# ScalarE's sigmoid visit per pair of heads in a gated linear recurrent layer, made in two parts one slot apart

## Chip, core and metric

One core of a Trainium2 chip runs the whole program: one launch, no other core busy. The metric is device time in microseconds (us). Engines: TensorE (PE; its weight loads are PEld), VectorE (DVE), ScalarE (ACT), GpSimd (POOL), and SyncE (SP), which only issues DMAs here.

## What is computed

A trunk of four layers with 384 token rows (256 of a prompt, 8 streams of 16). Each layer is a token mixer followed by a gated feed-forward net, both closed by a residual and a layer norm. The mixers are forgetting attention (layers 0 and 3), a gated linear recurrence (layer 1) and causal pooling (layer 2). The change lies in layer 1 alone:

```python
def hgrn_chunk_step(S, inp):
    q, k, v, g = inp
    b = jnp.cumsum(g, axis=1)
    decay = jnp.exp(jnp.where(causal, b[:, :, None] - b[:, None, :], -jnp.inf))
    scores = jnp.einsum('bthc,bshc,btshc->bhts', q, k, decay)
    o = jnp.einsum('bhts,bshv->bthv', scores, v) + jnp.einsum('bthc,bhcv->bthv', q * jnp.exp(b), S)
    S_new = jnp.exp(b_last)[..., None] * S + jnp.einsum('bshc,bshv->bhcv', k * jnp.exp(b_last[:, None] - b), v)

q, fx, iv, gate = jnp.split(x @ w_in, 4, axis=-1)
q = jax.nn.silu(q)
log_f = jnp.log(lb + (1.0 - lb) * jax.nn.sigmoid(fx))
k = (1.0 - lb) * jax.nn.sigmoid(-fx)
o = o * lax.rsqrt(jnp.mean(jnp.square(o), axis=-1, keepdims=True) + RMS_EPS) * norm_g
o = o.reshape(B, T, D_MODEL) * jax.nn.silu(gate)
return o @ w_out, S_final
```

There are 8 heads of 128 channels. For each pair of heads four sigmoids are wanted: of `q`, of `fx`, of `-fx`, and of `gate`; and one logarithm.

## The kernel before

Each engine runs a program of its own, written out by hand, and the programs meet only at semaphores. An engine works its list strictly in order, so a wait in it holds up everything behind it. The sets of functions for which ScalarE has tables differ: sigmoid is in one, logarithm and exponential in another, and each change of set is an `ACT_TABLE_LOAD` (copy and square run with either).

Weights stream through a ring of six buffers in units of 256 rows by 512 columns (`w_raw`, 128 x 1024). SyncE loads a unit when the unit six places ahead of it has been used (`unit_used`), ScalarE rounds it to `w_hi` (`w_hi_of`, L386), VectorE writes the rest to `w_lo` (`w_lo_of`, L676), and TensorE makes three products of them (`unit_fm`, `unit_tm`).

The recurrent layer (`hgrn`) runs in slots, a loop over `u` that every engine has (L579 of ScalarE, L1019 of VectorE, L1841 of TensorE). Slots 0 to 31 hold one unit of the input projection each, eight for each pair of heads `g`: four (`u % 8` below 4) for queries and forget values, four for values and gates. Beside them run the steps of the heads: head `h` begins its sums of logarithms in slot 6 + 4h and its products in slot 10 + 4h (`phases`). What the change and the prediction touch:

- **Slot 8g + 4.** ScalarE copies the queries to `q_g` (L586), VectorE the forget values to `f_r` (L1025). At the slot's end ScalarE runs `sigmoids(g)` (L513): the load of the sigmoid tables, the sigmoids of queries (`sg_q`), of forget values (`g_s`), of their negatives (`k_g`) and of the gates of the pair before (`sg_g`, from `g` = 1 on), the load of the log and exp tables, then two logarithms over `g_s`.
- **Slot 8g + 5.** VectorE runs `results(h)` for `h` = 2g - 2 (L992). It waits for the finished gate (L1005) and multiplies the head's output by it (L1008). Behind it in its list stand `sample_states`, then `state_sides(2g - 1)`, which writes `k2` (L946, L948), then `w_lo`, then the multiply of `q_g` by `sg_q` and of `k_g` by a constant (L1059, L1062). ScalarE runs two exponentials (L554) and one `w_hi`.
- **Slot 8g + 6.** TensorE opens with `turn_keys(2g - 1)` (L1765), which waits for `k2` (L1767), then `turn_logs(2g)`, which waits for the logarithms (L1738), then the slot's unit. ScalarE copies the turned logarithms to `gT_hi` (L595), VectorE subtracts them to `gT_lo` (L1045), and `sums` in slot 8g + 7 waits for both (L1749).
- **GpSimd** finishes gates in `gates(g)` (L1338): it waits for the semaphore `sgg` and makes two multiplies (L1342, L1345).
- In slot 33 `sigmoids(GRP)` makes the last pair's gate sigmoid alone.

Of the kernel before, what the change touches and what calls it, by code (L numbers as in the profile page):

```python
# [22 lines left out]
ACT = mybir.ActivationFunctionType  # L23
# [36 lines left out]
GRP = HG // 2  # L60
# [28 lines left out]
def trunk_program(nc, x_prompt, x_sample, cache_fox_k, cache_fox_v, cache_fox_lf, state_hgrn, cache_pool,  # L89
# [8 lines left out]
    with ExitStack() as ctx:  # L98
# [31 lines left out]
        lb_col = sb("lb_col", [P, KD], after("lbT"))  # L130
        oml_col = sb("oml_col", [P, KD], after("lb_col"))
# [135 lines left out]
        def at(mark, value):  # L267

            return mark[0], value + mark[1]
# [108 lines left out]
        def _(act):  # L378
# [131 lines left out]
            def hgrn(i, j):  # L510
                f, m0, out0 = HGR[i], START[i]["mix"], START[i]["out"]

                def sigmoids(g):  # L513

                    if g < GRP:
                        act.wait_ge(*at(f["f_ev"], g + 1))
                        act.wait_ge(*at(f["q_ev"], g + 1))
                        act.wait_ge(*at(f["qk"], g))
                        nc.scalar.activation(sg_q[:, :, :], q_g[:, g % 2, :, :], ACT.Sigmoid)
                        act.wait_ge(*at(f["gT"], 2 * g))  # L520
                        nc.scalar.activation(g_s[:, :, :], f_r[:, :, :], ACT.Sigmoid)
                        nc.scalar.activation(k_g[:, g % 2, :, :], f_r[:, :, :], ACT.Sigmoid, scale=-1.0).then_inc(f["sig"][0], 1)
                    if g:
                        act.wait_ge(*at(f["t01_ev"], g))
                        act.wait_ge(*at(f["t2_ev"], g))
                        act.wait_ge(*at(f["gate"], 2 * g - 2))
                        nc.scalar.activation(sg_g[:, :, :], gate[:, (g - 1) % 2, :, :], ACT.Sigmoid).then_inc(f["sgg"][0], 1)
                    log_exp_table()
                    if g < GRP:
                        act.wait_ge(*at(f["sig"], g + 1))  # L530
                        for e in range(2):
                            h = 2 * g + e
                            nc.scalar.activation(g_s[:, e, :], g_s[:, e, :], ACT.Ln, bias=lb_col[:, h:h + 1],
                                                 scale=oml_col[:, h:h + 1]).then_inc(f["g"][0], 1)

                def exps(h, first):

# [41 lines left out]
                for u in range(SLOTS):  # L579
                    (ha, ka), (hb, kb) = phases(u)  # L580
                    g = u // 8
                    if u % 8 == 4 and g < GRP:
                        act.wait_ge(unit_used, m0 + u)
                        if g >= 2:
                            act.wait_ge(*at(f["o"], 2 * g - 2))
                        nc.scalar.activation(q_g[:, g % 2, :, :], ps[:, FM_BANK[g]:FM_BANK[g] + 2, 0:T], ACT.Copy).then_inc(f["q_ev"][0], 1)  # L586
                    if u % 8 == 0 and 1 <= g <= GRP:
                        act.wait_ge(unit_used, m0 + u)
                        nc.scalar.activation(vo[:, 0:2, 2 * P * (g - 1):2 * P * g], ps[:, 4:6, 0:2 * P], ACT.Copy)
                        nc.scalar.activation(gate[:, (g - 1) % 2, 0:2, :], ps[:, 4:6, 2 * P:4 * P], ACT.Copy).then_inc(f["t01_ev"][0], 1)  # L590
                    if kb == 0:
                        turned_keys(hb)
                    if ka == 0:
                        act.wait_ge(*at(f["gT"], ha + 1))
                        nc.scalar.activation(gT_hi[:, :], ps[:, 0, 0:T], ACT.Copy).then_inc(f["gT_hi"][0], 1)  # L595
                    if kb == 2:
                        squares(hb)
                    if ka is not None and ka >= 1:
                        exps(ha, 2 * ka - 2)
                    for h in TURN_AT.get(u, ()):  # L600
                        turned_out(h)
                    if 1 <= u <= 8 * GRP:
                        w_hi_of(m0 + u - 1 + RING)
                    if u - 2 in OUT_AT:
                        w_hi_of(out0 + OUT_AT[u - 2] + RING)
                    if u % 8 == 4 and g < GRP:
                        sigmoids(g)
                    if u == 8 * GRP + 1:
                        sigmoids(GRP)
                turned_out(HG - 1)  # L610
                for u in range(len(OUT_AT), 2 * CU - TAIL):
                    w_hi_of(out0 + u + RING)
# [55 lines left out]
        def _(dve):  # L668
# [241 lines left out]
            def hgrn(i, j):  # L910
# [108 lines left out]
                for u in range(SLOTS):  # L1019
                    (ha, ka), (hb, kb) = phases(u)  # L1020
                    g = u // 8
# [32 lines left out]
                        w_lo_of(m0 + u - 1 + RING)  # L1054
                    if u - 2 in OUT_AT:
                        w_lo_of(out0 + OUT_AT[u - 2] + RING)
                    if u % 8 == 5 and g < GRP:
                        dve.wait_ge(*at(f["sig"], g + 1))
                        V.tensor_tensor(q_g[:, g % 2, :, :], q_g[:, g % 2, :, :], sg_q[:, :, :], ALU.mult)  # L1059
                        for e in range(2):  # L1060
                            h = 2 * g + e
                            ins = V.tensor_scalar(k_g[:, g % 2, e, :], k_g[:, g % 2, e, :], oml_col[:, h:h + 1], None, ALU.mult)  # L1062
                        ins.then_inc(f["qk"][0], 1)
# [102 lines left out]
        def _(pool):  # L1166
# [102 lines left out]
            def hgrn(i, j):  # L1269
# [67 lines left out]

                def gates(g):  # L1338

                    pool.wait_ge(*at(f["sgg"], g + 1))  # L1340
                    v = gate[:, g % 2, :, :]
                    G.tensor_tensor(v, v, sg_g[:, :, :], ALU.mult).then_inc(f["gate"][0], 1)  # L1342
                    pool.wait_ge(*at(f["gate"], 2 * g + 1))
# [610 lines left out]
```

## Time and profile before

| | us |
|---|---|
| Median of 3 runs | 2068.61 (2068.29 to 2070.44) |
| The profiled execution | 2065.23 |
| Its span, first to last instruction | 2063.5 |
| TensorE busy | 1910.4 (93%) |
| VectorE busy | 989.5 (48%) |
| ScalarE busy | 713.0 (35%) |
| GpSimd busy | 199.8 (10%) |

The granted clock of TensorE has a mean of 0.956 of 2.4 GHz. The recurrent layer's slots take about 594 to 845 us of the span. In the timeline's rows stand start and duration in us, the engine, the line of the kernel, the operation with output and inputs, the number of instructions merged in the row, and in brackets how long the engine had been idle before it and what ended that. A duration reaches to the end of an instruction's writing, and the next one may start a little earlier, so steps are best taken from start to start.

### The profile page before, as it was taken

To read this page: it belongs to the slowest core of one execution; us is meant where nothing else is said; L and a number is where in the kernel's file an instruction comes from. 1 tells how busy PE (TensorE), PEld (TensorE's weight loads), DVE (VectorE), ACT (ScalarE), POOL (GpSimd) and SP (SyncE) were. 2 spreads that over 40 slices of the span, in tenths; PEclk is the share of its full clock that TensorE was granted. 3 is DMA by queue.
4 is the path that set the end of the run, shared out by engine and by line. 5 is a ranking of instruction groups with operands and counts; after the bars stand their busy time and mean duration, and the time that the engine had idled before them with its cause. 6 is when DMAs were issued, how large, how long until landed. Compare 5 with 4: busy or idle time off the path is not lost.

```text
span 2063.5 us, 29582 instructions
## 1 busy us (share of the span) xinstructions
PE 1910.4 (93%) x12312; PEld 1726.7 (84%) x12312; DVE 989.5 (48%) x1568; ACT 713.0 (35%) x1123; POOL 199.8 (10%) x306
## 2 busy tenths in 40 slices
PE   5998999999989999799999559999999899999997
PEld 5878879998877887699998459998888688899985
DVE  3345463433456667733433673443444454534343
ACT  2235423333244544233332213333232353333331
POOL 4003200000051112100000100000030131000000
PEclk8999999999999999999999779999998899999998
DMA  6245334443353333334433324443362462444331
GB/s 216 87 152 186 133 120 126 125 131 123 107 150 93 115 107 96 104 122 123 127 128 123 102 65 129 123 133 123 104 207 86 154 208 97 133 123 129 126 125 70
DMA packets 179158, 259.45 MB, mean 126 GB/s; under 512 B 14669, under 2 KB 122333, under 8 KB 179024
## 3 DMA queue, kind: packets, MB, share of 16 engines
q1 hardware_dynamic: 160736, 195.61, 29.5%
q0 software_dynamic: 18288, 61.94, 9.1%
q8 instruction: 98, 1.61, 0.3%
q14 instruction: 36, 0.29, 0.0%
HBM read 243.20 MB, written 13.19 MB: 124 GB/s over the span
## 4 chain that ended last, share of the span: by engine, by line
PE 85%; DVE 7%; ACT 3%; DMA 2%; issue 1%; POOL 1%; SPq 0%; ACTq 0%; DVEq 0%; POOLq 0%
PE ps L1456 14%; PE ps L1458 14%; PE ps L1457 14%; PE ps L1467 10%; PE ps L1465 10%; PE ps L1466 10%; PE ps L1625 1%; PE ps L1701 1%; PE ps L1612 1%; DVE x_tok L755 1%; DVE xT_lo L695 1%; DMA w_raw<-in_w_fox_in_dram 1%; DVE x_tok L740 1%; PE ps L1684 1%; DVE w_lo L676 1%
## 5 line engine op out<-in xcount | busy, mean ns | idle before, releaser
L676 DVE TENSOR_TENSOR w_lo<-w_raw,w_hi 128x1024 fp32r<-128x1024 f32 x370 | 453.3, 1229 | 833.1 <-ACT w_hi L386 832.0
L386 ACT ACTIVATE w_hi<-w_raw 128x1024 fp32r<-128x1024 f32 x370 | 390.1, 1059 | 921.8 <-DMA w_raw<-in_w_ffn_in_dram 409.6
L1456 PE MATMUL ps<-xT_hi,w_hi 128*128 128x384 f32 x1664 | 566.5, 340 | 24.8 <-DVE xT_lo L695 23.6
L1457 PE MATMUL ps<-xT_lo,w_hi 128*128 128x384 f32 x1664 | 564.9, 339 | 0.0
L1458 PE MATMUL ps<-xT_hi,w_lo 128*128 128x384 f32 x1664 | 564.5, 339 | 0.0
L1456 PEld LDWEIGHTS ps<-xT_hi,w_hi 128*128 128x128 f32 x1664 | 317.5, 191 | 27.9 <-issue 26.0
L1457 PEld LDWEIGHTS ps<-xT_lo,w_hi 128*128 128x128 f32 x1664 | 317.4, 191 | 0.4
L1458 PEld LDWEIGHTS ps<-xT_hi,w_lo 128*128 128x128 f32 x1664 | 317.1, 191 | 0.0
L1467 PE MATMUL ps<-w_hi,hT_lo 128*128 128x512 f32 x528 | 210.7, 399 | 0.0
L1466 PE MATMUL ps<-w_lo,hT_hi 128*128 128x512 f32 x528 | 208.0, 394 | 0.0
L1465 PE MATMUL ps<-w_hi,hT_hi 128*128 128x512 f32 x528 | 207.3, 393 | 0.0
L1465 PE MATMUL ps<-w_hi,xT_hi 128*128 128x512 f32 x432 | 178.6, 413 | 4.0 <-issue 2.6
L1467 PE MATMUL ps<-w_hi,xT_lo 128*128 128x512 f32 x432 | 175.3, 406 | 0.0
L1466 PE MATMUL ps<-w_lo,xT_hi 128*128 128x512 f32 x432 | 174.6, 404 | 0.0
L1466 PEld LDWEIGHTS ps<-w_lo,hT_hi 128*128 128x128 f32 x528 | 99.1, 188 | 25.4
L1465 PEld LDWEIGHTS ps<-w_hi,hT_hi 128*128 128x128 f32 x528 | 99.1, 188 | 23.4
L1467 PEld LDWEIGHTS ps<-w_hi,hT_lo 128*128 128x128 f32 x528 | 99.1, 188 | 22.8
L1465 PEld LDWEIGHTS ps<-w_hi,xT_hi 128*128 128x128 f32 x432 | 84.2, 195 | 23.5 <-issue 3.3
L1467 PEld LDWEIGHTS ps<-w_hi,xT_lo 128*128 128x128 f32 x432 | 83.7, 194 | 20.4
L1466 PEld LDWEIGHTS ps<-w_lo,xT_hi 128*128 128x128 f32 x432 | 84.0, 194 | 19.1
L1171 POOL DMA_DIRECT2D gb<-in_ln_g_dram x8 | 4.4, 553 | 755.7 <-DVE x_tok L755 755.7
L1484 PE MATMUL ps<-ident,x_tok 128*128 128x128 f32 x192 | 34.2, 334 | 34.8 <-DVE x_tok L755 34.7
(301 smaller groups left out, 2003.2 us busy)
## 6 DMA issues: line engine op xcount, KB each, us to landing
w_raw<-in_w_ffn_in_dram SPq DMA_DIRECT2D x352, 256.0 KB, 3.2
w_raw<-in_w_ffn_out_dram SPq DMA_DIRECT2D x176, 256.0 KB, 2.8
w_raw<-in_w_fox_in_dram SPq DMA_DIRECT2D x96, 256.0 KB, 2.9
k_c<-in_cache_fox_k_dram POOLq DMA_DIRECT2D x32, 512.0 KB, 4.8
v_c<-in_cache_fox_v_dram POOLq DMA_DIRECT2D x32, 512.0 KB, 3.9
w_raw<-in_w_hgrn_in_dram SPq DMA_DIRECT2D x64, 256.0 KB, 3.0
w_raw<-in_w_fox_out_dram SPq DMA_DIRECT2D x32, 256.0 KB, 2.8
gb<-in_ln_g_dram POOLq DMA_DIRECT2D x8, 512.0 KB, 3.9
```

Source lines behind the costliest of these rows:

```text
L386: nc.scalar.activation(w_hi[:, slot, :], w_raw[:, slot, :], ACT.Copy).then_inc(hi_ready, 1)
L676: V.tensor_tensor(w_lo[:, slot, :], w_raw[:, slot, :], w_hi[:, slot, :].bitcast(F32), ALU.subtract).then_inc(lo_ready, 1)
L695: V.tensor_tensor(xT_lo[:, ks, tt], turned(n, t, hf)[1], xT_hi[:, ks, tt].bitcast(F32), ALU.subtract).then_inc(TR[n]["lo"][0], 1)
L740: V.scalar_tensor_tensor(out=x_tok[:, t, :], in0=x_tok[:, t, :], scalar=mv[:, t, 0:1], in1=gb[:, 0, :], op0=ALU.subtract, op1=ALU.mult).th ...
L755: V.scalar_tensor_tensor(out=x, in0=x, scalar=r, in1=gb[:, 1, cols], op0=ALU.mult, op1=ALU.add).then_inc(ln["x"][0], 1)
L1456: mm(out, w_hi[:, slot, cols], x_hi[:, k, :], start=k == 0, stop=False)
L1457: mm(out, w_hi[:, slot, cols], x_lo[:, k, :], start=False, stop=False)
L1458: last = mm(out, w_lo[:, slot, cols], x_hi[:, k, :], start=False, stop=k == KD - 1)
L1465: mm(out, x_hi[:, k, tt], w_hi[:, slot, cols], start=k == 0, stop=False)
L1466: mm(out, x_hi[:, k, tt], w_lo[:, slot, cols], start=False, stop=False)
L1467: return mm(out, x_lo[:, k, tt], w_hi[:, slot, cols], start=False, stop=k == nk - 1)
L1484: ins = nc.tensor.transpose(out[:, k, :], x_tok[:, t, c:c + P], ident[:, :])
```

## The change

`sigmoids(g)` is made two functions. `logs(g)` stays at the end of slot 8g + 4 and holds the two sigmoids of the forget values and the two logarithms. `gate_sigmoids(g)` is run at the end of slot 8g + 5 and holds the sigmoid of the queries and that of the gates of the pair before. Each brings both table loads with it. `sgg` is now raised in every visit, the first included, so GpSimd waits for one more of it. VectorE multiplies `q_g` and `k_g` a slot later, and waits for `sgg` too.

```diff
--- before.py
+++ after.py
@@ -510,28 +510,32 @@
             def hgrn(i, j):
                 f, m0, out0 = HGR[i], START[i]["mix"], START[i]["out"]
 
-                def sigmoids(g):
+                def logs(g):
+
+                    act.wait_ge(*at(f["f_ev"], g + 1))
+                    act.wait_ge(*at(f["gT"], 2 * g))
+                    nc.scalar.activation(g_s[:, :, :], f_r[:, :, :], ACT.Sigmoid)
+                    nc.scalar.activation(k_g[:, g % 2, :, :], f_r[:, :, :], ACT.Sigmoid, scale=-1.0).then_inc(f["sig"][0], 1)
+                    log_exp_table()
+                    act.wait_ge(*at(f["sig"], g + 1))
+                    for e in range(2):
+                        h = 2 * g + e
+                        nc.scalar.activation(g_s[:, e, :], g_s[:, e, :], ACT.Ln, bias=lb_col[:, h:h + 1],
+                                             scale=oml_col[:, h:h + 1]).then_inc(f["g"][0], 1)
+
+                def gate_sigmoids(g):
 
                     if g < GRP:
-                        act.wait_ge(*at(f["f_ev"], g + 1))
                         act.wait_ge(*at(f["q_ev"], g + 1))
                         act.wait_ge(*at(f["qk"], g))
-                        nc.scalar.activation(sg_q[:, :, :], q_g[:, g % 2, :, :], ACT.Sigmoid)
-                        act.wait_ge(*at(f["gT"], 2 * g))
-                        nc.scalar.activation(g_s[:, :, :], f_r[:, :, :], ACT.Sigmoid)
-                        nc.scalar.activation(k_g[:, g % 2, :, :], f_r[:, :, :], ACT.Sigmoid, scale=-1.0).then_inc(f["sig"][0], 1)
+                        ins = nc.scalar.activation(sg_q[:, :, :], q_g[:, g % 2, :, :], ACT.Sigmoid)
                     if g:
                         act.wait_ge(*at(f["t01_ev"], g))
                         act.wait_ge(*at(f["t2_ev"], g))
                         act.wait_ge(*at(f["gate"], 2 * g - 2))
-                        nc.scalar.activation(sg_g[:, :, :], gate[:, (g - 1) % 2, :, :], ACT.Sigmoid).then_inc(f["sgg"][0], 1)
+                        ins = nc.scalar.activation(sg_g[:, :, :], gate[:, (g - 1) % 2, :, :], ACT.Sigmoid)
+                    ins.then_inc(f["sgg"][0], 1)
                     log_exp_table()
-                    if g < GRP:
-                        act.wait_ge(*at(f["sig"], g + 1))
-                        for e in range(2):
-                            h = 2 * g + e
-                            nc.scalar.activation(g_s[:, e, :], g_s[:, e, :], ACT.Ln, bias=lb_col[:, h:h + 1],
-                                                 scale=oml_col[:, h:h + 1]).then_inc(f["g"][0], 1)
 
                 def exps(h, first):
 
@@ -604,9 +608,11 @@
                     if u - 2 in OUT_AT:
                         w_hi_of(out0 + OUT_AT[u - 2] + RING)
                     if u % 8 == 4 and g < GRP:
-                        sigmoids(g)
+                        logs(g)
+                    if u % 8 == 5 and g < GRP:
+                        gate_sigmoids(g)
                     if u == 8 * GRP + 1:
-                        sigmoids(GRP)
+                        gate_sigmoids(GRP)
                 turned_out(HG - 1)
                 for u in range(len(OUT_AT), 2 * CU - TAIL):
                     w_hi_of(out0 + u + RING)
@@ -1054,8 +1060,9 @@
                         w_lo_of(m0 + u - 1 + RING)
                     if u - 2 in OUT_AT:
                         w_lo_of(out0 + OUT_AT[u - 2] + RING)
-                    if u % 8 == 5 and g < GRP:
+                    if u % 8 == 6 and g < GRP:
                         dve.wait_ge(*at(f["sig"], g + 1))
+                        dve.wait_ge(*at(f["sgg"], g + 1))
                         V.tensor_tensor(q_g[:, g % 2, :, :], q_g[:, g % 2, :, :], sg_q[:, :, :], ALU.mult)
                         for e in range(2):
                             h = 2 * g + e
@@ -1337,7 +1344,7 @@
 
                 def gates(g):
 
-                    pool.wait_ge(*at(f["sgg"], g + 1))
+                    pool.wait_ge(*at(f["sgg"], g + 2))
                     v = gate[:, g % 2, :, :]
                     G.tensor_tensor(v, v, sg_g[:, :, :], ALU.mult).then_inc(f["gate"][0], 1)
                     pool.wait_ge(*at(f["gate"], 2 * g + 1))
```

ScalarE, slots 12 and 13 (`g` = 1), the list before:

```order
L519 ACT_TABLE_LOAD
L519 ACTIVATE sg_q<-q_g 128x768
L521 ACTIVATE g_s<-f_r 128x768
L522 ACTIVATE k_g<-f_r 128x768
L527 ACTIVATE sg_g<-gate 128x768
L425 ACT_TABLE_LOAD
L533 ACTIVATE g_s<-g_s,lb_col,oml_col 128x384 x2
L554 ACTIVATE lev<-ps 128x512 x2
L386 ACTIVATE w_hi<-w_raw 128x1024
L559 ACTIVATE k2T<-ps 128x384
```

And the same place in the changed kernel, whose first five rows are slot 12 (its lines are up to six higher):

```order
L517 ACT_TABLE_LOAD
L517 ACTIVATE g_s<-f_r 128x768
L518 ACTIVATE k_g<-f_r 128x768
L425 ACT_TABLE_LOAD
L523 ACTIVATE g_s<-g_s,lb_col,oml_col 128x384 x2
L558 ACTIVATE lev<-ps 128x512 x2
L386 ACTIVATE w_hi<-w_raw 128x1024
L531 ACT_TABLE_LOAD
L531 ACTIVATE sg_q<-q_g 128x768
L536 ACTIVATE sg_g<-gate 128x768
L425 ACT_TABLE_LOAD
L563 ACTIVATE k2T<-ps 128x384
```

The gate's sigmoid stood in the fifth row, ahead of the second table load; it now stands in the tenth, behind that load, the logarithms, the exponentials, the copy to `w_hi` and a third load. The fourth load stands ahead of `k2T` and `gT_hi`. In slots 4 and 5 the order is the same without `sg_g`, and `gT_hi` follows the fourth load at once.

VectorE, from the output multiply of slot 13 to the first row of slot 15, before (L676 is `w_lo`, L923 a row of `low_sides`, L948 writes `k2`, L960 opens slot 15):

```order
L1008 SCALAR_TENSOR_TENSOR vo<-ps,rr,gate 128x128 x3
...
L948 TENSOR_TENSOR k_125<-k_g,c_123 128x128
...
L676 TENSOR_TENSOR w_lo<-w_raw,w_hi 128x1024
L1059 TENSOR_TENSOR q_g<-q_g,sg_q 128x768
L1062 TENSOR_SCALAR k_g<-k_g,oml_col 128x384 x2
L923 TENSOR_TENSOR lev<-lev,k_g 128x3x64
...
L1045 TENSOR_TENSOR gT_lo<-ps,gT_hi 128x384
L676 TENSOR_TENSOR w_lo<-w_raw,w_hi 128x1024
L960 COPY s_135<-ps 128x128
```

And in the changed kernel:

```order
L1014 SCALAR_TENSOR_TENSOR vo<-ps,rr,gate 128x128 x3
...
L954 TENSOR_TENSOR k_125<-k_g,c_123 128x128
...
L682 TENSOR_TENSOR w_lo<-w_raw,w_hi 128x1024
L929 TENSOR_TENSOR lev<-lev,k_g 128x3x64
...
L1051 TENSOR_TENSOR gT_lo<-ps,gT_hi 128x384
L682 TENSOR_TENSOR w_lo<-w_raw,w_hi 128x1024
L1066 TENSOR_TENSOR q_g<-q_g,sg_q 128x768
L1069 TENSOR_SCALAR k_g<-k_g,oml_col 128x384 x2
L966 COPY s_135<-ps 128x128
```

What stands between the output multiply and the write of `k2` is unchanged; the multiplies of `q_g` and `k_g` moved from slot 13's end to slot 14's.

## Rows read from the trace of the kernel before

**Rows 1.** Page, part 4: shares of the chain that ended last.

```profile
PE 85%; DVE 7%; ACT 3%; DMA 2%; issue 1%; POOL 1%; SPq 0%; ACTq 0%; DVEq 0%; POOLq 0%
```

**Rows 2.** Waits of TensorE, then VectorE, in the recurrent layer (us, times, longest).

```profile
PE ps L1770 <- DVE k L948: 6.7, 3, 2.2
...
DVE vo L1008 <- POOL gate L1345: 19.8, 3, 6.6
```

**Rows 3.** Timeline of ScalarE, slots 12 and 13: start, duration, instruction, idle before.

```profile
650.45 1.28 ACT L519 ACT_TABLE_LOAD   x1
651.74 0.84 ACT L519 ACTIVATE sg_q<-q_g 128x768 f32<-128x768 f32 x1
652.50 0.83 ACT L521 ACTIVATE g_s<-f_r 128x768 f32<-128x768 f32 x1
653.23 0.83 ACT L522 ACTIVATE k_g<-f_r 128x768 f32<-128x768 f32 x1
653.96 0.83 ACT L527 ACTIVATE sg_g<-gate 128x768 f32<-128x768 f32 x1
654.81 1.28 ACT L425 ACT_TABLE_LOAD   x1
656.11 1.31 ACT L533 ACTIVATE g_s<-g_s,lb_col,oml_col 128x384 f32<-128x384 f32 x2
657.32 1.06 ACT L554 ACTIVATE lev<-ps 128x512 f32<-128x512 f32 x2
658.27 1.05 ACT L386 ACTIVATE w_hi<-w_raw 128x1024 fp32r<-128x1024 f32 x1
```

**Rows 4.** Timeline of VectorE, slot 13: the output multiply and the write of `k2`.

```profile
658.75 0.87 DVE L1008 SCALAR_TENSOR_TENSOR vo<-ps,rr,gate 128x128 f32<-128x128 f32 x3 [6.59 <-POOL gate L1345]
...
660.90 0.28 DVE L948 TENSOR_TENSOR k<-k_g,c 128x128 f32<-128x128 f32 x1
```

**Rows 5.** Timeline of GpSimd, slot 13: the second of the two gate multiplies.

```profile
656.79 1.85 POOL L1345 TENSOR_TENSOR gate<-gate,ng 128x768 f32<-128x768 f32 x1
```

**Rows 6.** Timeline of TensorE, slots 13 and 14.

```profile
652.85 1.02 PE L1830 MATMUL ps<-v_m,k2T 128*128 128x512 f32 x2
...
658.36 0.39 PE L1466 MATMUL ps<-w_lo,xT_hi 128*128 128x512 f32 x1
658.60 0.40 PE L1467 MATMUL ps<-w_hi,xT_lo 128*128 128x512 f32 x1
661.24 0.55 PE L1770 MATMUL ps<-ident,k 128*128 128x128 f32 x3 [2.25 <-DVE k L948]
...
663.36 0.63 PE L1465 MATMUL ps<-w_hi,xT_hi 128*128 128x512 f32 x1
663.78 0.63 PE L1466 MATMUL ps<-w_lo,xT_hi 128*128 128x512 f32 x1
```

**Rows 7.** Stretches: bounds, length, busy of PE, PEld, DVE, ACT, POOL, PEclk, DMA.

```profile
661.20:665.40 4.20, 4.16 (x15) 3.43 (x16) 4.20 (x12) 1.92 (x3) 0.86 (x1) 0.59 0.57 177
779.00:783.00 4.00, 4.00 (x21) 3.35 (x22) 4.00 (x12) 1.82 (x3) 0.53 (x1) 1.00 0.54 166
158.70:163.50 4.80, 4.06 (x16) 3.48 (x16) 1.31 (x3) 0.70 (x2) 3.67 (x6) 0.50 0.69 272
30.60:33.60 3.00, 2.94 (x9) 2.97 (x10) 0.79 (x2) 0.00 (x0) 0.00 (x0) 0.50 0.00 0
```

**Rows 8.** Timeline, slots 6 and 7: ScalarE, VectorE, TensorE.

```profile
610.12 0.49 ACT L595 ACTIVATE gT_hi<-ps 128x384 fp32r<-128x384 f32 x1
613.15 1.06 ACT L386 ACTIVATE w_hi<-w_raw 128x1024 fp32r<-128x1024 f32 x1 [2.54 <-DMA w_raw<-in_w_hgrn_in_dram]
...
612.77 0.55 DVE L1045 TENSOR_TENSOR gT_lo<-ps,gT_hi 128x384 fp32r<-128x384 f32 x1
...
609.60 0.49 PE L1741 MATMUL ps<-ident,g_s 128*128 128x128 f32 x3
...
614.12 0.39 PE L1761 MATMUL ps<-wsum,gT_hi 128*128 128x512 f32 x1
```


## The prediction

> **What bounds the kernel now.** I read the shares of the last chain first: 85% of it is TensorE [rows 1], so an edit on the other engines counts only where TensorE waits for them. The list of waits inside the recurrent layer comes next. TensorE waits there for one line of VectorE above all, L948, which writes `k2`: three times, 2.2 us at most, 6.7 in all. VectorE in turn waits three times for GpSimd's gate, 19.8 us in all [rows 2]. Three is the number of visits that hold a gate's sigmoid in the slots with weights (`g` = 1, 2, 3), and the timeline shows that the waits form one chain.
>
> The first of the three places stands in the rows. ScalarE starts its first table load at 650.45; the gate's sigmoid starts at 653.96 and ends at 654.79, with three sigmoids ahead of it [rows 3]. GpSimd's two multiplies follow, the second ending at 658.64 [rows 5]. VectorE, idle for 6.59, starts the output multiply at 658.75 and ends `k2` at 661.18 [rows 4]. TensorE's last product started at 658.60; it turns the keys at 661.24, after 2.25 idle [rows 6]. So at this place TensorE has no slack against the gate's sigmoid: it is waiting already, and what delays that sigmoid delays everything behind it one for one.
>
> **The gate's sigmoid, later.** The changed order of ScalarE, priced from start to start by [rows 3], from the same 650.45: table load and its gap 1.29; `g_s` 0.76 (as the first sigmoid behind a load now has), `k_g` 0.85 (as the last sigmoid ahead of a load has): the second load starts at 653.35. Load 1.30, two logarithms 1.21, two exponentials 0.95: the copy to `w_hi` starts at 656.81. The copy takes 1.05, and 0.03 to the next load: 657.89. Load 1.29, queries' sigmoid 0.76, gate's sigmoid 0.83: it ends at 660.77, against 654.79. That is 5.98 later. Two of the items are table loads that the visit did not have ahead of the gate; the rest is work that stood behind it. Behind the sigmoid nothing changes up to TensorE: two gate multiplies, the output multiply, `sample_states`, the two writes of `k2`. So TensorE's idle stretch grows from 2.25 to 8.2. Three places give 3 x 5.98 = **17.9 us**.
>
> This copy to `w_hi` now stands ahead of the gate's sigmoid and brings its own condition, a loaded weight unit, and so SyncE's queue. Before, it started at 658.27 with no wait, so the unit had landed by then. If it landed no earlier, each place loses 1.46 more, 4.4 in all. The nearest case says it lands sooner: the unit that is released when slot 5 ends (609.60) is copied from 613.15 on, after a wait for DMA, 3.55 later [rows 8]. Slot 12's unit has its end at 652.85 [rows 6]; plus 3.55 this is 656.40, and ScalarE arrives at 656.81. I take 0, and keep 4.4 as the far end; it cannot go below 0, since the 656.81 is ScalarE's own work.
>
> **The clock.** After the idle stretch of 2.25 TensorE runs at its lower level, 1.2 GHz: a granted clock of 0.59 over 4.20 us [rows 7] is (1 - 0.59) / 0.5 x 4.20 = 3.4 us at half. The second place reads the same and the third stays at 1.00 [rows 7], so 6.9 us in all. After longer idle stretches (7.8 us before 158.70, 17.4 before 30.60) it stays at 0.50 for 4.8 and 3.0 us of work [rows 7]. The change makes all three stretches that long. With the middle, 3.9, this makes 11.7 us at half, 4.8 more than now. A product of 512 columns starts 0.42 after the last at half, 0.24 at full [rows 6], so 43% of that time is lost: **2.1 us**, between 0.9 (three times 3.0) and 3.2 (three times 4.8).
>
> **The first visit (`g` = 0).** It has no gate. Its query sigmoid and two loads now come at the end of slot 5, ahead of `gT_hi`. Before, `gT_hi` started at 610.12, VectorE's `gT_lo` at 612.77, and `sums` at 614.12 behind work of TensorE's own [rows 8]. Load 1.29, sigmoid 0.85, load 1.30 put `gT_hi` at 613.56; with its 0.49, VectorE's 0.55 and 0.1 for the two handovers `sums` starts at 614.70: **0.6 us** of new wait. It is 0 if the handovers run closer, and no gain. In the other three visits the fourth load stands ahead of `k2T` and `gT_hi` but ends at about 662.1, when TensorE has not yet turned the keys; it costs nothing there.
>
> **Edits taken at nothing.** The logarithms end 1.46 earlier (their start moves from 656.11 to 654.65), but `turn_logs` stands behind `turn_keys`, which now comes at 667.2. The multiplies of `q_g` and `k_g` leave VectorE's slot 13 for the end of slot 14: both places lie behind the write of `k2` and ahead of slot 15, so what VectorE has done by slot 15 is the same. `high_sides`, which needs them, comes two slots later. VectorE's rows behind the gate's wait, `w_lo` of slot 13 among them, are 6 us late too; TensorE stands still for the same 6 us, so none of them is late against it. GpSimd's stores and loads of the states hang on VectorE's steps and move with them. Slot 33 keeps its order.
>
> Sum: 17.9 + 2.1 + 0.6 = 20.6 us. The profiled execution's own time is 2065.23 (span 2063.5 and 1.7 around it), so its like would be 2085.8. The median of the runs shown is 2068.61, 3.4 above it; the difference is carried over, and I forecast **2089.2 us**.
>
> **A rule against the row.** ScalarE's load starts 0.02 after the sigmoid ahead of it has ended (654.79 to 654.81), lasts 1.28, and the logarithm starts 0.02 behind it [rows 3]: 1.3 us in all. The sum above rests on that. The Trainium skill ("ScalarE: Activation LUTs", What ACT_TABLE_LOAD costs) gives the same 1283 ns but adds about 1380 ns of draining for every switch. This case's trace shows no such gap.
>
> **Rivals.**
> 1. *Loads cost more than the row shows*, because a load placed behind a copy empties the engine for as long again. There are eight new loads, two in each visit; 8 x 1.28 = 10.2 more would give 2099.4. By the page's 1.38 it would be 11.0, an estimate. Against it: the load row. Chance 0.03.
> 2. *Part of the delay is taken in*: TensorE gets behind the gate in only two of the three places, or waits that it would have had later in the layer shrink. A place is worth 6.0 + 0.7 for the clock, so 2082.5. Against it: TensorE is idle at all three places already. Chance 0.04.
> 3. *Faster.* TensorE's wait in front of the turned keys is in truth for the logarithms, whose transposes come right behind. Then the earlier logarithms give 3 x 1.46 = 4.4, and 2064.2. It decides where the gate's sigmoid would end before 654.79, or be wanted more than 6 us later than the trace has it. Against it: the logarithms end at 657.42, 3.8 before TensorE resumes, while `k2` ends 0.06 before. Chance 0.02.
> 4. *No visible effect* (within 0.2%, which is 4.1 us and about what a measurement of this kernel can tell): the gate could be wanted later than VectorE's list says. Chance 0.02.
> 5. *Slower still* than the bounds reach, by a late weight unit and a later restart of the clock together: 0.02.
>
> **How the numbers follow.** The forecast has the other 0.87. From the bounds: the low end is 17.9 + 0.9 = 18.8, and with a microsecond off for each of the handovers and the spread of runs some 17, so 2085.5; the high end is 17.9 + 3.2 + 0.6 + 4.4 = 26.1, so 2094.7, rounded to 2095. Slower by over 0.2%: 0.87 + 0.03 + 0.04 + 0.02 = 0.96; within: 0.02; faster: 0.02.
>
> **What the profile of the changed kernel would show.** TensorE's wait for `k2` near 24 us over three places, about 8.2 each. VectorE's wait for the gate near 12.5 at each. ScalarE's gate sigmoid ending some 10.3 after the visit's first load began, with the `w_hi` copy between running without a wait for DMA, or with a short one. A clock of 0.5 for 3 to 5 us behind each of the three. One new wait of about half a microsecond at the first `sums`. The rest of the program unchanged to the microsecond. If the wait for `k2` stays near 2.25, or moves to the logarithms, the argument is wrong at its root; if it is 8 and the total moves by less than 15 us, something later gives time back.

## The result, and the profile after

The changed kernel takes 2095.2 us, the median of 4 runs (2092.58 to 2097.37); the kernel before takes 2069.53, the median of 4 beside it (2068.29 to 2070.59). The ratio is 1.0121, with a 95% interval from 1.0105 to 1.0138. On the 2068.61 us that the prediction started from, this is +25.0 us (21.7 to 28.5), or 2093.6 us. The forecast was +20.6, 2089.2 us, with a range from 2085.5 to 2095.0. So the direction is right, the time by the ratio is inside the range and near its upper end, and the bare median stands 0.2 us above it. The cause is the one that was forecast; about 4 us of the size are not in its sum.

The shares of the last chain (the page's part 4, changed kernel) look like those of [rows 1]. A loss of 1.2% can't be seen in them:

```profile
PE 84%; DVE 7%; ACT 3%; DMA 2%; issue 2%; POOL 1%; SPq 0%; ACTq 0%; DVEq 0%; POOLq 0%
```

It is in the waits. The first two lines answer [rows 2]; the last is new. This is the list of waits of the changed kernel in the recurrent layer: engine, line waited for, us in all, times, longest.

```profile
DVE vo L1014 <- POOL gate L1352: 37.3, 3, 12.4
...
PE ps L1777 <- DVE k L954: 24.3, 3, 8.1
...
PE ps L1768 <- DVE gT_lo L1051: 0.5, 1, 0.5
```

TensorE still waits three times for `k2`, but for 8.1 us each time where it was 2.2 (L1777 was L1770). The timeline of ScalarE in the changed kernel, which answers [rows 3], shows why. Its columns are start, duration, instruction, idle before:

```profile
654.09 1.28 ACT L517 ACT_TABLE_LOAD   x1
655.39 0.84 ACT L517 ACTIVATE g_s<-f_r 128x768 f32<-128x768 f32 x1
656.14 0.83 ACT L518 ACTIVATE k_g<-f_r 128x768 f32<-128x768 f32 x1
656.98 1.28 ACT L425 ACT_TABLE_LOAD   x1
658.28 1.31 ACT L523 ACTIVATE g_s<-g_s,lb_col,oml_col 128x384 f32<-128x384 f32 x2
659.49 1.05 ACT L558 ACTIVATE lev<-ps 128x512 f32<-128x512 f32 x2
660.45 1.05 ACT L386 ACTIVATE w_hi<-w_raw 128x1024 fp32r<-128x1024 f32 x1
661.51 1.28 ACT L531 ACT_TABLE_LOAD   x1
662.81 0.84 ACT L531 ACTIVATE sg_q<-q_g 128x768 f32<-128x768 f32 x1
663.56 0.83 ACT L536 ACTIVATE sg_g<-gate 128x768 f32<-128x768 f32 x1
664.40 1.28 ACT L425 ACT_TABLE_LOAD   x1
671.67 0.49 ACT L563 ACTIVATE k2T<-ps 128x384 f32<-128x384 f32 x1 [5.98 <-PE ps L1777]
```

From the visit's first load to the end of the gate's sigmoid it is 664.39 - 654.09 = 10.30 us; before it was 654.79 - 650.45 = 4.34. The copy to `w_hi` at 660.45 carries no wait for DMA, nor do the copies at the other two places (724.74 and 790.74). The third load, which stands behind that copy, takes 662.81 - 661.51 = 1.30 us to the next sigmoid, like every other. The fourth load, at 664.40, is followed by 5.98 us in which ScalarE waits for TensorE, so it costs nothing.

What follows the sigmoid, on GpSimd and TensorE of the changed kernel (the answer to [rows 5] and [rows 6]):

```profile
666.34 1.80 POOL L1352 TENSOR_TENSOR gate<-gate,ng 128x768 f32<-128x768 f32 x1
```

```profile
617.88 0.47 PE L1768 MATMUL ps<-wsum,gT_hi 128*128 128x512 f32 x1 [0.51 <-DVE gT_lo L1051]
...
670.73 0.90 PE L1777 MATMUL ps<-ident,k 128*128 128x128 f32 x3 [8.09 <-DVE k L954]
...
801.02 0.90 PE L1777 MATMUL ps<-ident,k 128*128 128x128 f32 x3 [8.10 <-DVE k L954]
...
902.00 0.66 PE L1463 MATMUL ps<-xT_hi,w_hi 128*128 128x384 f32 x1 [0.77 <-DVE xT_lo L701]
```

From the end of the gate's sigmoid to the turned keys it is 670.73 - 664.39 = 6.34 us; before, 661.24 - 654.79 = 6.45. That part is untouched, and of the sigmoid's 5.96 us of delay 5.84 arrive as idle of TensorE (8.09 - 2.25).

The stretches behind the three waits, in the changed kernel (bounds, length, busy time of PE, PEld, DVE, ACT, POOL, granted clock, DMA), answer [rows 7]. The fourth row is the end of the recurrent layer, the fifth an up-projection of a feed-forward block (FFN):

```profile
670.73:675.50 4.77, 4.77 (x16) 4.07 (x17) 4.77 (x14) 1.93 (x3) 1.38 (x2) 0.57 0.39 115
735.00:739.80 4.80, 4.78 (x15) 4.03 (x16) 4.80 (x14) 1.93 (x3) 0.82 (x1) 0.51 0.36 109
801.00:804.60 3.60, 3.58 (x12) 3.10 (x13) 3.60 (x12) 1.93 (x3) 0.66 (x1) 0.51 0.51 150
866.30:876.00 9.70, 8.33 (x18) 5.55 (x19) 2.82 (x10) 0.49 (x1) 0.90 (x1) 0.50 0.18 54
906.30:1091.00 184.70, 184.70 (x1045) 184.70 (x1045) 70.93 (x64) 61.63 (x64) 0.00 (x0) 1.00 0.40 123
```

The last two have these counterparts in the kernel before:

```profile
841.50:847.80 6.30, 4.72 (x18) 3.16 (x19) 2.77 (x10) 0.49 (x1) 0.90 (x1) 1.00 0.28 83
877.50:1060.00 182.50, 182.50 (x1053) 182.18 (x1052) 72.59 (x65) 62.08 (x65) 0.00 (x0) 1.00 0.40 125
```

TensorE's whole idle is the length of the layer less its busy time. The layer is taken here from its first `sums` to the first product of the feed-forward block behind it, first in the kernel before, then in the changed one:

```profile
614.12:873.79 259.67, 236.57 (x2312) 194.60 (x2311) 176.68 (x424) 112.23 (x217) 51.03 (x40) 0.97 0.33 101
```

```profile
617.88:902.00 284.12, 243.45 (x2312) 199.25 (x2312) 181.14 (x428) 120.67 (x223) 52.87 (x40) 0.91 0.30 92
```

The idle grows from 259.67 - 236.57 = 23.1 to 284.12 - 243.45 = 40.7, so by 17.6 us, which is what the three waits for `k2` grow by: the other waits of the layer, taken together, neither shrink nor grow. The same number of products is busy 6.9 us longer, at a granted clock of 0.91 where it was 0.97.

**Where the time went.** The two spans differ by 2093.7 - 2063.5 = 30.2 us. I cut them at the same two places. Ahead of the first cut there are 3.8 us, of which 0.5 is the new wait at `sums`. Between the cuts it is 259.67 before and 284.12 after, 24.4 more: 17.6 of idle (24.3 - 6.7), 2.5 of clock at the three restarts, and 4.3 of the rest, most of it at the end of the layer, where the same 18 products take 6.30 us at a clock of 1.00 in one profile and 9.70 at 0.50 in the other. Behind the second cut there are 2.0 more, made of 3.6 in the one up-projection (0.177 us from product to product in place of 0.173, at a granted clock of 1.00 both times, over 1045 products) less what other parts gave back. Only the idle, the clock at the restarts and the half microsecond stood in the forecast. Whether the rest belongs to the change was the main open question.

### The profile page after: what moved, and what is told of

Same layout as the page of the kernel before. It is cut to its first block, busy times and chain, and to the rows that moved or that the text cites. A ratio compares the mean times of both kernels' runs of the same rounds, so it can differ in the third digit from the quotient of the medians.

```text
span 2093.7 us, 29598 instructions
## 1 busy us (share of the span) xinstructions
PE 1925.2 (92%) x12312; PEld 1739.2 (83%) x12312; DVE 993.6 (47%) x1568; ACT 723.9 (35%) x1131; POOL 202.4 (10%) x306
## 4 chain that ended last, share of the span: by engine, by line
PE 84%; DVE 7%; ACT 3%; DMA 2%; issue 2%; POOL 1%; SPq 0%; ACTq 0%; DVEq 0%; POOLq 0%
PE ps L1463 14%; PE ps L1464 14%; PE ps L1465 14%; PE ps L1472 10%; PE ps L1474 10%; PE ps L1473 10%; PE ps L1632 1%; PE ps L1708 1%; PE ps L1619 1%; DVE x_tok L761 1%; DVE xT_lo L701 1%; DMA w_raw<-in_w_fox_in_dram 1%; DVE x_tok L746 1%; PE ps L1691 1%; ACT w_hi L386 1%
## 5 line engine op out<-in xcount | busy, mean ns | idle before, releaser
L1463 PE MATMUL ps<-xT_hi,w_hi 128*128 128x384 f32 x1664 | 568.7, 342 | 24.1 <-DVE xT_lo L701 23.1
L1474 PEld LDWEIGHTS ps<-w_hi,hT_lo 128*128 128x128 f32 x528 | 99.1, 188 | 23.6
L1472 PEld LDWEIGHTS ps<-w_hi,hT_hi 128*128 128x128 f32 x528 | 99.2, 188 | 23.1
```

The costliest lines, as they stand in the source:

```text
L1463: mm(out, w_hi[:, slot, cols], x_hi[:, k, :], start=k == 0, stop=False)
L1472: mm(out, x_hi[:, k, tt], w_hi[:, slot, cols], start=k == 0, stop=False)
L1474: return mm(out, x_lo[:, k, tt], w_hi[:, slot, cols], start=False, stop=k == nk - 1)
```

## The experiments

**Theory.** TensorE is tied to the end of the gate's sigmoid: gate multiplies on GpSimd, the output multiply on VectorE, `k2` behind it in VectorE's list, the turned keys. What the sigmoid loses, TensorE loses in three places, plus a slower clock behind each. **Rivals.** The two further table loads of each visit cost more than their row; the turned keys wait for the logarithms; the multiplies of `q_g` and `k_g`, moved behind `low_sides`, cost or give something; what isn't in the sum is an effect of the change that the theory lacks.

Each run below was timed beside the kernel before. Its medians there were 2072.9 (22 runs) for the first four, 2072.89 (29 runs) for the next four and 2072.22 (13 runs) for the last. Single runs of it spread from 2064.77 to 2082.16. "Stretch" is the time from the first `sums` to the first FFN product in the profile, as above.

**The changed kernel again** (no edit).

> The changed kernel unaltered, for its spread. The sum explains 21 us over the kernel before; its first profile shows 30 in the span, 22 of them in the recurrent layer, the rest in other layers, where no instruction moved (TensorE longer at 1.2 GHz, and one feed-forward net whose products start 0.177 us apart instead of 0.173). Theory A, that rest is chance from run to run: a median between 2090 and 2096, and another profile in which the other layers lie within 3 us of the kernel before. Theory B, the change brings it about: again 2095 and the same extra stretches in the same layers. Both: three waits of 8.1 us for k2.

2097.36 us (6 runs), ratio 1.0114 [1.0089, 1.0139], which is +23.6 us. TensorE's waits for `k2` are 24.3 us over three places again, the stretch is 284.00. So the idle repeats with the order; the total repeats within its interval, though the median lies above both theories' 2095 to 2096. Outside the stretch this profile takes 1808.3 us, where the first profile of before took 1803.8 and its second, below, 1809.3: the rest in the other layers is not the change's (theory A). The slow end of the recurrent layer came again, which the next run answers.

**The kernel before again** (no edit), to see what of the first comparison was its own.

> The kernel before, unaltered, for a second profile. In both profiles of the changed kernel and in that of two more table loads, the stretch from the last state update of the recurrent layer through its out projection's first six products (6.3 us in the first profile of before) is 3.3 us longer, at 1.2 GHz. Theory A, the first profile of the kernel before was a lucky one: the second shows that stretch 2 to 6 us longer too, and the wait for k2 again 6.7. Theory B, the longer idle stretches bring it about: the stretch is 6.3 again. Time: ratio 0.998 to 1.002.

2071.24 us (10 runs), ratio 0.9994 [0.9976, 1.0012]. Theory A holds. The waits are the same 6.7 us, but the stretch is 264.38 where the first profile had 259.67, with the same code. Two rows of this second profile show where: behind the third wait and at the layer's end.

```profile
778.60:782.40 3.80, 3.66 (x13) 3.19 (x14) 3.80 (x11) 1.93 (x3) 0.78 (x1) 0.56 0.64 201
847.00:856.00 9.00, 8.39 (x24) 6.67 (x25) 1.48 (x3) 0.00 (x0) 0.87 (x1) 0.63 0.20 58
```

Both places had a clock of 1.00 in the first profile ([rows 7], second row, and the 841.50 row above). On the timeline of TensorE, the third wait and the first FFN product stand as follows, first in the first profile of before, then in the second:

```profile
778.89 0.55 PE L1770 MATMUL ps<-ident,k 128*128 128x128 f32 x3 [2.25 <-DVE k L948]
...
873.79 0.66 PE L1456 MATMUL ps<-xT_hi,w_hi 128*128 128x384 f32 x1 [0.65 <-DVE xT_lo L695]
```

```profile
778.74 0.90 PE L1770 MATMUL ps<-ident,k 128*128 128x128 f32 x3 [2.25 <-DVE k L948]
...
879.33 0.66 PE L1456 MATMUL ps<-xT_hi,w_hi 128*128 128x384 f32 x1 [0.82 <-DVE xT_lo L695]
```

From the one to the other it is 94.90 us in the first profile of before, 100.59 in the second, 100.98 in the changed kernel (801.02 to 902.00). The slow end of the layer therefore doesn't need the change: the second profile of before has it too, and the first was one without it. Nor do long waits for `k2` bring it of themselves: the kernel with the second visit earlier (below) has three of 6.2 us, and its layer ends as fast as in the first profile of before, the same 18 products in 6.30 us at a clock of 1.00:

```profile
860.70:867.00 6.30, 4.73 (x18) 3.15 (x19) 2.76 (x10) 0.49 (x1) 0.90 (x1) 1.00 0.28 83
```

Against the second profile of before, the changed kernel's stretch is 284.12 - 264.38 = 19.7 us longer. That is the 17.6 of idle, 1.0 of clock (0.3, 0.6 and 0.1 at the three places) and 1.1 unexplained. The slower pace of an up-projection is there without the change too, in another layer. The same 140 us in the first profile of before, then in the second:

```profile
1260.00:1400.00 140.00, 140.00 (x810) 140.00 (x809) 58.05 (x52) 49.79 (x52) 0.00 (x0) 1.00 0.41 127
```

```profile
1260.00:1400.00 140.00, 140.00 (x794) 140.00 (x794) 55.00 (x49) 48.20 (x50) 0.00 (x0) 1.00 0.41 124
```

TensorE gets through 810 products in the one and 794 in the other, without a pause in either.

**Two more loads ahead of the gate's sigmoid**, in the kernel before, which otherwise keeps its order. The gate waits for two loads more and for nothing else. The logarithms come later by the same loads, but end at 665.67, 3.8 us before TensorE resumes (669.43).

```
                         act.wait_ge(*at(f["gate"], 2 * g - 2))
+                        if g < GRP:
+                            log_exp_table()
                         nc.scalar.activation(sg_g[...], gate[...], ACT.Sigmoid).then_inc(...)
```

> The kernel before, with the log and exp tables loaded and the sigmoid tables loaded again between k_g and the gate's sigmoid, at the three visits that hold a gate in the slots with weights; nothing else moves. Theory, 1.29 us for a load and nothing behind it: the gate is 2.6 later, TensorE's idle stretches are 4.8 each, 7.7 in all and 1 to 2.5 for the clock: 2077.5 to 2080. Rival, a load costs its length again in draining: the stretches are 7.4 each and the time 2086 or more.

2086.65 us (7 runs), ratio 1.0069 [1.0048, 1.0091]. ScalarE's timeline and TensorE's wait in this kernel:

```profile
655.99 1.28 ACT L519 ACT_TABLE_LOAD   x1
...
659.62 1.28 ACT L425 ACT_TABLE_LOAD   x1
660.90 1.28 ACT L529 ACT_TABLE_LOAD   x1
662.20 0.84 ACT L529 ACTIVATE sg_g<-gate 128x768 f32<-128x768 f32 x1
```

```profile
PE ps L1772 <- DVE k L950: 14.7, 3, 4.9
```

Two loads take 662.20 - 659.62 = 2.58 us, and each of the waits grows by 2.65. A load costs its row and no more: the rival wanted waits of 7.4. The total alone wouldn't have told. It grew by 14.3 us (9.9 to 18.9), of which the longer waits are 8.0; the theory had 9 to 11 over the 2068.6 it started from, the rival 17 or more, and the interval reaches into both.

**The second visit at the start of ScalarE's slot** in place of its end, in the changed kernel: the four loads stay, the exponentials and the copy to `w_hi` no longer stand ahead of the gate.

```
+                    if u % 8 == 5 and g < GRP:
+                        gate_sigmoids(g)
                     if kb == 0:
                         turned_keys(hb)
...
-                    if u % 8 == 5 and g < GRP:
-                        gate_sigmoids(g)
```

> The changed kernel with the second visit at the start of ScalarE's slot 8g + 5, ahead of its two exponentials and its copy to w_hi. The gate's sigmoid then ends 8.3 after the first load's start, against 10.3 in the changed kernel and 4.3 in the kernel before. Theory, one for one: idle stretches of 2.25 + 3.95 = 6.2 us, three times, and no wait at the first sums (the query sigmoid then lies in ScalarE's wait for DMA): 12 us over the kernel before for the waits, and 1.5 to 6 for the clock, ratio 1.006 to 1.009. Rival, the changed kernel's loss is ScalarE's list as a whole (loads, order of exponentials): no better than the change, 1.011 or more.

2086.69 us (4 runs), ratio 1.007 [1.0042, 1.0097]. The theory's ratio (1.006 to 1.009) and wait (6.2) both came true, and the rival (1.011 or more) is excluded. The wait fell as the sigmoid came earlier:

```profile
PE ps L1777 <- DVE k L954: 18.6, 3, 6.2
...
655.34 1.28 ACT L517 ACT_TABLE_LOAD   x1
...
662.90 0.83 ACT L536 ACTIVATE sg_g<-gate 128x768 f32<-128x768 f32 x1
```

**The gate's sigmoid in the first visit, only the queries' in the second**, in the changed kernel. All eight further loads stay, and the logarithms and multiplies stay where the change put them. (`gate_sigmoid` and `query_sigmoid` are `gate_sigmoids` cut in two, each with its own semaphore.)

```
                     nc.scalar.activation(k_g[...], f_r[...], ACT.Sigmoid, scale=-1.0)...
+                    if g:
+                        gate_sigmoid(g)
                     log_exp_table()
...
                     if u % 8 == 5 and g < GRP:
-                        gate_sigmoids(g)
+                        query_sigmoid(g)
```

> The change with one thing undone: the gate's sigmoid stays in the first visit (slot 8g + 4), behind those of the forget values, and only the queries' sigmoid moves to the second, with its two table loads. All eight new loads are there. Theory, only the gate's place counts: it ends 3.61 after the visit's start instead of 4.34, so TensorE's idle stretches are 1.5 us instead of 2.25; 0.5 new wait in the first visit: 2064 to 2068.5. Rival, the second visit costs by its loads and by ScalarE's time: 2080 or more.

2068.09 us (12 runs), ratio 0.9974 [0.9956, 0.9991]: faster than before, though only just by the interval. The whole loss of the change is gone, with all its loads in place:

```profile
PE ps L1780 <- DVE k L957: 4.6, 3, 1.5
...
651.97 1.28 ACT L517 ACT_TABLE_LOAD   x1
...
654.75 0.83 ACT L533 ACTIVATE sg_g<-gate 128x768 f32<-128x768 f32 x1
```

Each fence shows the wait, the visit's first load and the gate's sigmoid. With these, the wait can be set against the time from the visit's first load to the end of the gate's sigmoid, read from ScalarE's timeline in the same way everywhere:

| kernel | sigmoid ends behind the first load (us) | against before | wait for `k2` per place | against before |
|---|---|---|---|---|
| gate in the first visit | 3.61 | -0.73 | 1.5 | -0.7 |
| before | 4.34 | | 2.25 | |
| before, two more loads | 7.05 | +2.71 | 4.9 | +2.65 |
| change, second visit earlier | 8.39 | +4.05 | 6.2 | +3.95 |
| change | 10.30 | +5.96 | 8.1 | +5.85 |

Four edits of different kinds give one line, one for one within 0.11 us. It makes no difference whether the sigmoid is late by loads, by exponentials or by a copy.

**The multiplies of `q_g` and `k_g` a slot later**, alone, in the kernel before.

```
-                    if u % 8 == 5 and g < GRP:
+                    if u % 8 == 6 and g < GRP:
                         dve.wait_ge(*at(f["sig"], g + 1))
```

> The kernel before with the change's smallest part alone: VectorE multiplies q_g and k_g at the end of slot 8g + 6 instead of 8g + 5; ScalarE's list is untouched. Theory, both places lie behind the write of k2 and ahead of slot 8g + 7: the wait for k2 stays 6.7 us, no new wait, ratio 0.998 to 1.002. Rival, the multiplies now run beside GpSimd's v_m or ahead of the join and delay the scores: a wait of TensorE for VectorE's scores of 1 to 2 us in three places, ratio 1.002 to 1.004.

2073.13 us (10 runs), ratio 1.001 [0.9994, 1.0027], and the wait is that of before:

```profile
PE ps L1770 <- DVE k L948: 6.8, 3, 2.3
```

This part of the change costs nothing that can be measured, as the prediction took it.

**Results behind the sides of the state**, in the kernel before. It leaves ScalarE alone and cuts the chain at another link: VectorE writes `k2` first and waits for the gate afterwards.

```
                     if kb == 3:
-                        results(hb)
                         sample_states(hb, 1)
...
                     if ka == 3:
                         state_sides(ha)
+                    if kb == 3:
+                        results(hb)
```

> The kernel before, with VectorE's output multiply (results) put behind the write of k2 in slots 8g + 5, so that the gate is no longer between ScalarE and TensorE; ScalarE's list is untouched. Theory, TensorE waits for k2 only because the gate's wait stands ahead of it in VectorE's list: the three idle stretches of 2.25 us go (6.7) and with them most of the 6.9 us at 1.2 GHz (3.0): 2059 to 2063. Rival, TensorE waits for the logarithms or for VectorE's load of work: the idle stretches stay, on another line, 2068 to 2070.

2062.97 us (6 runs), ratio 0.9943 [0.9918, 0.9969], 11.8 us less than the kernel before beside it (6.4 to 17.0). TensorE's wait for `k2` is gone from its list. At the first place VectorE has written `k2` (L948, ending 660.37) when TensorE comes to the turned keys at 660.42, and the output multiply (L1008) comes only then. The margin there is thin, 0.05 us. The first fence is VectorE, the second GpSimd, the third TensorE:

```profile
656.45 2.06 DVE L946 TENSOR_TENSOR k<-k_g,lev 128x256 f32<-128x256 f32 x1
658.43 1.94 DVE L948 TENSOR_TENSOR k<-k_g,c 128x128 f32<-128x128 f32 x1
...
661.34 0.87 DVE L1008 SCALAR_TENSOR_TENSOR vo<-ps,rr,gate 128x128 f32<-128x128 f32 x3
```

```profile
656.38 1.84 POOL L1343 TENSOR_TENSOR gate<-gate,sg_g 128x768 f32<-128x768 f32 x1 [15.04 <-ACT sg_g L527]
658.30 1.92 POOL L1346 TENSOR_TENSOR gate<-gate,ng 128x768 f32<-128x768 f32 x1
```

```profile
660.42 0.55 PE L1771 MATMUL ps<-ident,k 128*128 128x128 f32 x3
```

It shows that `k2` had no need of the gate: it only stood behind a wait for it. What comes late next is the output multiply at the layer's end, for which TensorE waits 3.2 us in two places where it waited 0.2 in one before. The 11.8 us are thus 3.7 of idle saved (6.7 less 3.0). The rest is the work at 1.2 GHz that no longer follows those waits, for which the expectation took 3.0, and chance; this run doesn't part them.

```profile
PE ps L1839 <- DVE vo L1008: 3.2, 2, 2.6
```

**The same edit on the changed kernel.** If the chain through `results` is the whole cause, most of the loss goes.

> The changed kernel with VectorE's output multiply behind the write of k2. Theory: the wait for k2 goes, but the gate now comes 6 us later than VectorE is ready for it, and behind its wait stand w_lo and low_sides, for which TensorE waits in the middle of slot 8g + 7: 2 to 3.5 us each, on that line: ratio 0.997 to 1.001. Rival, nothing behind the gate is near TensorE's path: no new wait and 0.993 to 0.996, as without the change. Rival, the two visits cost by themselves: 1.008 or more.

2080.41 us (10 runs), ratio 1.0035 [1.0019, 1.0052]. The wait for `k2` is gone, but not the delay. First VectorE, then TensorE's list of waits:

```profile
669.44 0.87 DVE L1014 SCALAR_TENSOR_TENSOR vo<-ps,rr,gate 128x128 f32<-128x128 f32 x3 [8.19 <-POOL gate L1353]
```

```profile
PE ps L1813 <- DVE lev L930: 9.3, 4, 2.9
```

VectorE still stands 8.19 us at the gate, now behind `k2`, and the next thing in its list that TensorE wants, `lev` of `low_sides`, comes 2.9 us late at three places. The expectation had the line and the size of this wait (2 to 3.5 us) but a better ratio, 0.997 to 1.001; it had left out the 3.2 us of wait for the output multiply, which this edit brings here as in the kernel before. Beside the kernel before, the loss falls from 25.0 to 7.3 us. But the edit makes that kernel itself 11.8 us faster. With late results in both, the change still costs 0.0092 of the time (0.006 to 0.012), some 19 us, and in the profiles the stretch is 268.11 us with the change and 254.14 without. So most of the loss stays: it has moved from one wait to another. The gate's lateness is too great for one row moved in VectorE's list to hide it.

**Both cures together** (gate in the first visit, results behind the sides).

> The gate's sigmoid in the first visit, the queries' alone in the second, and VectorE's output multiply behind the write of k2: the edits of two earlier runs together (ratios 0.9974 and 0.9943 alone). Theory, the late multiply has already taken the gate off TensorE's path, so an earlier gate adds nothing: 0.993 to 0.996. Rival, the gains add: 0.990 to 0.993.

2063.98 us (12 runs), ratio 0.9961 [0.9947, 0.9974], no wait for `k2`, at the edge of the theory and clear of the rival. It isn't better than the late results alone. The two edits remove the same idle, so their gains don't add.

The late results on the kernel before have the lowest ratio found and beat both kernels. From both cures together they can't be told apart, as the intervals overlap.

## Why the prediction was right, and where its size was off

**The chain: right, and shown.** TensorE's idle at the three places was forecast as 8.2 us each and measured as 8.09 to 8.10; the sigmoid was to end 10.32 behind the first load and ended 10.30 behind it; VectorE's wait for the gate was to be 12.5 and is 12.4. The idle term was 17.9 and is 17.6. The table of the five kernels makes this more than an agreement in one number.

**The copy to `w_hi`: right.** It was taken at 0 with 4.4 as the far end; none of the three rows has a wait for DMA.

**The first visit: right.** 0.6 forecast, 0.51 measured.

**Edits taken at nothing: right** for the fourth load (5.98 us of ScalarE's idle behind it), for the logarithms (they end at 659.5, 11 us ahead of the turned keys, and nothing gets faster by it) and for the late multiplies (ratio 1.001 alone).

**The clock: right at the restarts, too narrow elsewhere.** The restarts were forecast at 2.1 and measured at 2.5 against the first profile of before; 1.6 of this is the third place, which in the second profile of before was slow already; against that profile it is 1.0. That the forecast lies between the two is in part luck of the profile it started from. (The 0.59 that it reads at the second place stands in no row of [rows 7]; over 719.30 to 723.50 the trace does have it.) The step that failed is the sentence that the rest of the program would stay unchanged to the microsecond. It took one execution's pattern of granted clock for a property of the kernel. In fact the layer's end is at 1.00 in one profile of before and at 0.63 in the other, and a whole up-projection runs 3 to 4 us slower in some profiles, the second of before too, without a lower granted clock. The error was of size only: each such place is worth 3 to 4 us, beside 25 for the change.

**Rivals.** Loads that cost more than their row (2099.4) are excluded by the two-load run, 1.29 us a load with the gap included, and for a load behind a copy by the changed kernel's own row (1.30). The Trainium skill ("ScalarE: Activation LUTs", What ACT_TABLE_LOAD costs) adds about 1380 ns of draining for each switch; no row of these runs has it, and the measurement decides. Part of the delay taken in (2082.5): all three places lost the full 5.85, and the layer's whole idle grew by as much as these three. Logarithms as the true wait (2064.2): excluded, since they come earlier now and TensorE waits longer. No visible effect, and slower still: neither.

**What stays open.** By the ratio the change costs 25.0 us (21.7 to 28.5), in the repeat 23.6 (18.4 to 28.8); the terms found are 17.6 + 0.5 + 1.0 to 2.5, so 19.1 to 20.6. The 3 to 6 us between are not new waits and not in other layers. In the stretch TensorE's idle is 23.1 us in both profiles of before and 40.7 and 41.1 in the two of the changed kernel; its busy time, for the same products, is 236.6 and 241.3 against 243.5 and 242.9. So the products of this layer ran slower by 1.6 to 6.9 us, of which 1.0 to 2.5 are the restarts. What is open is why the rest was slow: chance, since the slow end of the layer is there in one profile of before and absent with waits of 6.2 us, or a tendency of longer idle stretches to leave more slow places behind them. Two profiles of each kernel don't tell these apart. The two-load kernel, with 14.3 for 8.0 of longer waits, points to the second, though its interval (9.9 to 18.9) reaches nearly down to it; the gate-first kernel, which has all the change's loads and is faster than before, shows at least that loads and moved work don't carry it.

## What to carry to other kernels

On an engine that works through a list in order, a wait delays all that stands behind it, so look there for a write that the busiest engine wants and that doesn't need what is waited for: here moving one call behind another gave 0.57% (0.31 to 0.82). It doesn't make the order safe against any delay: with the gate 6 us late, the change still cost some 19 us, by what stands next in the list. Before work is put ahead of something, find out what slack its last reader has; where the busiest engine already waited for the end of that chain, each microsecond was passed on one for one, and cheap-looking work (a load, a copy) cost its full length at every place. Before a few microseconds of difference between two profiles are explained, profile the old kernel twice.

## What the hardware showed that I had not expected

- **VectorE beside GpSimd.** In the kernel with late results, VectorE's two writes of `k2` run beside GpSimd's two gate multiplies and take 2.06 and 1.94 us (rows above, and the same again at the second place). In the kernel before, behind them, they took 0.42 and 0.28 ([rows 4] has the second). Each lasts about as long as the GpSimd instruction beside it (1.84 and 1.92). Without that, `k2` would be ready some 3.3 us ahead of TensorE at the first place, an estimate from these durations; with it the margin is 0.05. The edit pays all the same, since TensorE's list has no wait for them.
- **A short idle is enough for the clock to fall, mostly.** After TensorE's 2.25 us of idle a stretch of some 3.4 us at 1.2 GHz follows in five of the six places of the two profiles of before; in the sixth (779.00, [rows 7]) it doesn't.
- **Two paces at one granted clock.** The 384-column products of an up-projection follow each other 0.173 us or 0.177 us apart, over the 183 and 185 us of the rows above, at a granted clock of 1.00 both times. I found no cause in the trace.
